# A hybrid attention and mixture-of-experts block on one core: twelve weight places, a loop over pairs of experts, and the second bias added in one piece

## The chip, the cores and the metric

The kernel runs on one core of one Trainium2 chip. The metric is the device time of one execution in microseconds (us); the median of the runs counts. A difference below 0.3%, some 3.3 us, can't be told from no change with runs of this kernel.

## The reference

The block has a front (two token mixers: causal pooling and sparse attention, gated and added to the input) and a mixture of experts over its result, followed by a last RMS norm with a gain. 256 tokens, width 1024, 32 experts, each token goes to 4 of them. The change lies in the experts:

```python
def moe(h, w_router, b_router, w1, b1, w2, b2):
    logits = hf @ w_router + b_router
    top_vals, top_idx = lax.top_k(logits, TOP_K_EXPERTS)
    gates = jax.nn.softmax(top_vals, axis=-1)
    combine = jnp.sum(jax.nn.one_hot(top_idx, N_EXPERTS) * gates[..., None], axis=1)
    out = jnp.zeros((b * s, d), jnp.float32)
    for e in range(N_EXPERTS):
        gu = hf @ w1[e] + b1[e]                      # w1[e]: 1024 x 2048, w2[e]: 1024 x 1024, float32
        g_ = jnp.minimum(gu[:, :D_FF], SWIGLU_LIMIT)
        u_ = jnp.clip(gu[:, D_FF:], -SWIGLU_LIMIT, SWIGLU_LIMIT)
        act = g_ * jax.nn.sigmoid(SWIGLU_ALPHA * g_) * (u_ + 1.0)
        out = out + combine[:, e:e + 1] * (act @ w2[e] + b2[e])
```

The weights of all experts are read whatever the router says: 32 times 12.58 MB, 402.7 MB of the 436 MB that the kernel reads.

## The kernel before, in words

**Experts as steps.** The tokens of an expert are gathered into 64 slots (one-hot columns from the router, times the tokens, on PE), so that an expert is 64 rows against its weights. Its weights come as 12 steps of 1 MB: 8 of the first matrix (`w1`, 8 MB, line 1517 on PE) and 4 of the second (`w2`, 4 MB, line 1566). Two steps are a chunk of 2 MB, and each chunk goes to a place in SBUF. PE counts `chunks_used` up by one when it is through a step.

**Between the two matrices** PE has small work while DVE and ACT make the activations of the expert (clamp, sigmoid, product): the transposes of the slot columns (1534), the gathering of half of the next pair's tokens (`gather`, 1404), the transposes of the activations (1547), the bias of the next first matrix (`bias1`, 1360). Behind the second matrix of every second expert, results go back from slots to tokens (`scatter`, lines 1149 to 1151): three products of f32r halves, high by high, low by high, high by low, for 4 blocks, 12 matmuls for a pair. The gate is in the slot columns `gpick` that the scatter uses. The second bias `b2` is added by one matmul of 32 rows (1526) in each of the first four experts, through `combT`, the transposed gates of the tokens, and `b2s`.

**Transfers.** All weights come through SP's queue, in the order of use. SP waits until PE has used the chunk that lies in a place, and then issues the next chunk for it, so each transfer is issued when its place comes free:

```python
sp.wait_ge(chunks_used, 2 * plan[c][2] + 2)
chunk(c // CHUNKS, c % CHUNKS, place[plan[c][0]], chunk_loaded[plan[c][0]])
```

There are 11 places of 2 MB. The first 12 experts (72 chunks) are written out, on every engine, in 2 MB chunks. Behind them SP loads `gfin`, the gain of the last norm, broadcast to all partitions (512 KB). Then a loop takes the 16 experts of groups 3 to 6, in transfers of 4 MB into 4 quads (16 MB), of which each is two places. The last group of 4 experts is written out again, in 2 MB chunks; the last expert's chunks are partly halved.

**The last expert** has an order of its own (`last_expert`): its first matrix at line 1460, its activations in two halves, its second matrix by columns at 1481, its scatter at 1488. Then come the sums of squares, the last norm and the output.

## Time and profile before

| | |
|---|---|
| runs, us | 1091.92, 1090.02, 1088.32; median 1090.02 |
| profiled execution, us | 1088.94 (1.08 below the median) |
| its span, us | 1087.2 (1.7 below its own time) |
| busy | PE 94%, DVE 30%, ACT 19%, POOL 1% |
| DMA over the span | 403 GB/s mean, 437.88 MB |

Times in rows and text are us from the start of the span. The front fills the first 175 us or so, the experts the rest, and the last 8.0 us, from the end of the last scatter, are the norm and the output.

### The profile page before, as it was taken

The numbers are of one execution on the slowest core, as the hardware profiler recorded it, in microseconds if no ns is written. First come the engines' busy times: TensorE is split into PE (matmuls) and PEld (weight loads), VectorE is DVE, ScalarE is ACT, GpSimd is POOL, SyncE is SP. The second block draws the span as 40 slices with busy tenths as digits, with TensorE's granted clock in tenths as the row PEclk, the third lists the DMA queues.
The fourth block names the chain that finished last, engine by engine and source line by source line (L and its number), as shares of the span: only waits on it lengthen the run. The fifth ranks groups of instructions, "written<-read, shape, count | busy, mean of one in ns | idle before, by whom it ended". The sixth has DMA issues, their size and how long they took to land.

```text
span 1087.2 us, 12200 instructions
## 1 busy us (share of the span) xinstructions
PE 1021.8 (94%) x4995; PEld 502.9 (46%) x4995; DVE 328.7 (30%) x724; ACT 201.2 (19%) x343; POOL 10.8 (1%) x14
## 2 busy tenths in 40 slices
PE   9999999999999999999989899898989898999896
PEld 7987785334343434343434343434343343434342
DVE  6966574222222222222122222121121221121223
ACT  6565642101110111011101110110010100110012
POOL 0000020000000000000000000000000000000000
PEclk9999999999999999999999999999999999999999
DMA  8786769999999999999999999999999999999994
GB/s 339 272 351 254 289 258 386 396 433 430 428 433 430 430 430 429 432 431 438 427 435 432 433 435 433 435 432 435 428 436 429 434 434 434 433 428 429 428 430 178
DMA packets 29719, 437.88 MB, mean 403 GB/s; under 512 B 4616, under 2 KB 5296, under 8 KB 7664
## 3 DMA queue, kind: packets, MB, share of 16 engines
q1 hardware_dynamic: 29392, 436.80, 94.9%
q8 instruction: 29, 0.48, 0.2%
q10 hardware_dynamic: 288, 0.52, 0.1%
q14 instruction: 10, 0.08, 0.0%
HBM read 436.26 MB, written 2.11 MB: 403 GB/s over the span
## 4 chain that ended last, share of the span: by engine, by line
PE 74%; DMA 21%; DVE 2%; issue 1%; ACT 1%; POOL 0%; SPq 0%; ACTq 0%; DVEq 0%; POOLq 0%
PE bank L1517 30%; DMA quad<-in_w 18%; PE bank L1566 15%; PE bank L1149 6%; PE bank L1150 5%; PE bank L1151 5%; PE bank L1404 3%; DMA place<-in_w 3%; PE bank L1360 1%; PE bank L1460 1%; PE bank L1547 1%; PE bank L1481 1%; PE bank L1306 0%; PE bank L1526 0%; PE bank L1488 0%
## 5 line engine op out<-in xcount | busy, mean ns | idle before, releaser
L1517 PE MATMUL bank<-quad,r 128*64 128x512 f32 x1024 | 236.9, 620 | 20.3 <-DMA quad<-in_w 20.2
L1517 PE MATMUL bank<-place,r 128*64 128x512 f32 x960 | 210.4, 594 | 5.2 <-DMA place<-in_w 5.2
L1517 PEld LDWEIGHTS bank<-quad,r 128*64 128x64 f32 x1024 | 79.8, 142 | 167.7 <-issue 163.1
L1026 DVE TENSOR_SCALAR r<-bank 128x512 f32<-128x512 f32 x32 | 22.1, 692 | 398.3 <-PE bank L1517 386.0
L1517 PEld LDWEIGHTS bank<-place,r 128*64 128x64 f32 x960 | 67.4, 137 | 137.9 <-issue 130.1
L1566 PE MATMUL bank<-quad,r 128*64 128x512 f32 x512 | 113.4, 595 | 8.6 <-issue 5.5
L1057 DVE TENSOR_TENSOR ysl<-bank,ysh 64x512 fp32r<-64x512 f32 x62 | 42.7, 689 | 254.9 <-ACT ysh L697 253.9
L1566 PE MATMUL bank<-place,r 128*64 128x512 f32 x480 | 106.3, 594 | 7.7 <-issue 7.0
L682 ACT ACTIVATE r<-r 128x512 f32<-128x512 f32 x31 | 19.6, 632 | 453.5 <-DVE r L1026 453.5
L697 ACT ACTIVATE ysh<-bank 64x512 fp32r<-64x512 f32 x62 | 36.6, 591 | 225.5 <-PE bank L1566 224.7
L749 DVE TENSOR_TENSOR wl<-ring,wh 128x1024 fp32r<-128x1024 f32 (+1 forms) x52 | 64.0, 1241 | 37.4 <-ACT wh L526 36.9
L1566 PEld LDWEIGHTS bank<-quad,r 128*64 128x64 f32 x512 | 40.8, 137 | 72.1 <-issue 72.1
L1566 PEld LDWEIGHTS bank<-place,r 128*64 128x64 f32 x480 | 39.6, 137 | 65.8 <-issue 65.1
L1404 PEld LDWEIGHTS bank<-rt,hs 128*128 128x128 f32 x528 | 61.5, 192 | 13.7 <-issue 12.9
L1404 PE MATMUL bank<-rt,hs 128*128 128x128 f32 x528 | 66.1, 278 | 0.0
L526 ACT ACTIVATE wh<-ring 128x1024 fp32r<-128x1024 f32 (+1 forms) x52 | 53.7, 1042 | 55.1 <-PE bank L1151 53.2
L1149 PE MATMUL bank<-wh,hTh 128*128 128x512 f32 x96 | 39.0, 406 | 0.0
L1150 PE MATMUL bank<-wl,hTh 128*128 128x512 f32 x96 | 37.6, 392 | 0.0
L1151 PE MATMUL bank<-wh,hTl 128*128 128x512 f32 x96 | 37.4, 390 | 0.0
L1547 PE MATMUL bank<-cst,r 128*128 128x128 f32 x124 | 19.4, 279 | 12.1 <-DVE r L1040 12.1
L691 ACT ACTIVATE r<-bank 128x512 f32<-128x512 f32 x31 | 18.5, 597 | 61.7 <-PE bank L1547 61.7
L1063 DVE TENSOR_TENSOR r<-bank,gcol 128x512 f32<-128x512 f32 x32 | 22.1, 691 | 23.2 <-PE bank L1404 22.6
(227 smaller groups left out, 851.2 us busy)
## 6 DMA issues: line engine op xcount, KB each, us to landing
quad<-in_w SPq DMA_DIRECT2D x48, 4096.0 KB, 29.4
place<-in_w SPq DMA_DIRECT2D x93, 2048.0 KB, 21.5
ring<-in_w_front SPq DMA_DIRECT2D x24, 1024.0 KB, 5.4
place<-in_w SPq DMA_DIRECT2D x2, 1024.0 KB, 33.7
place<-in_w_last SPq DMA_DIRECT2D x1, 2048.0 KB, 35.0
place<-in_w_last SPq DMA_DIRECT2D x2, 1024.0 KB, 33.7
ring<-in_w_idx SPq DMA_DIRECT2D x4, 384.0 KB, 5.5
xs<-in_x SPq DMA_DIRECT2D x2, 512.0 KB, 8.8
```

Source lines behind the costliest of these rows:

```text
L526: nc.scalar.activation(piece_cols(wh[n % LOOK], n), ring_piece(n), ACT.Copy).then_inc(high_ready, 1)
L697: nc.scalar.activation(ysh[own, c, :], YT[c * SLOTS:(c + 1) * SLOTS, :], ACT.Copy)\
L749: nc.vector.tensor_tensor(piece_cols(wl[n % LOOK], n), ring_piece(n), piece_cols(wh[n % LOOK], n).bitcast(f32), ALU.subtract)\
L1026: nc.vector.tensor_scalar(gclip, GA[:, :], LIMIT, None, ALU.min).then_inc(gclip_ready, 1)
L1057: nc.vector.tensor_tensor(ysl[c][own, :], YT[c * SLOTS:(c + 1) * SLOTS, :], ysh[own, c, :].bitcast(f32), ALU.subtract).then_inc(y_low, 1)
L1149: mm(o, ah, bh, start=start and first_in_bank, stop=False, skip_group_check=True)
L1150: mm(o, ah, bl, start=False, stop=False, skip_group_check=True)
L1151: return mm(o, al, bh, start=False, stop=stop, skip_group_check=True)
L1404: ins = mm(bk[:, k * P:(k + 1) * P], hs[:, b, d], pick[:, b, :], start=b == 0, stop=b == TB - 1)
L1517: ins = mm(bk[part, :], xgT[i // 2 % 2][:, k, own], w[:, c1:c1 + HALF], start=False, stop=k == KD - 1)
L1547: ins = nc.tensor.transpose(GA[:, c * P:(c + 1) * P], act[:, c * P:(c + 1) * P], ident)
L1566: ins = mm(YT[part, :], a_k, w[:, kk, c1:c1 + HALF], start=k == 0, stop=k == KD - 1)
```

## The change

- **Places and transfers.** Another layout of SBUF gives 12 places (24 MB), two to each of 6 quads. The first pair of experts comes in chunks of 2 MB, the pairs 1 to 14 in a loop with 4 MB transfers, on every engine; in the last pair, expert 30 has three transfers of 4 MB and expert 31 ten of 2, 1 and 0.5 MB (its first matrix by columns: `w1_last`). A transfer of 4 MB waits until its four steps are free (`place_free`).
- **Gain of the last norm.** The broadcast of 512 KB is gone from SP's queue. ACT's queue loads one row of 4.6 KB during the last pair, and two matmuls of one row (`final_factors`) spread it over the partitions.
- **Slots and gates.** The slot columns `pick` no longer hold the gate: PE makes the gate of each slot with eight matmuls of one column (`slot_gates`), and DVE multiplies it into the activations. The scatter then takes 4 matmuls an expert, with the high and low halves of the result stacked in 128 rows, between the matrices of the next expert.
- **Second bias.** All of it (8 matmuls of 32 rows by 256 columns, `second_bias`) stands in expert 0, between its matrices.
- **Order on PE.** `gather(0)` stands in the second expert of a pair ahead of the second matrix, `gather(1)` and the two first biases behind it. There is one buffer `xgT` in place of two. The transposed activations go to ACT in two halves.
- **Last expert.** Activations in two halves of columns, a scatter of 8 matmuls in f32r, first biases in float32 (`last_bias`).

```diff
-PLACES = 11
-GROUP = 4
-GROUPS = NE // GROUP
+PLACES = 12
 PAIRS = NE // 2
-QUADS = 4
-TURNS = GROUP * STEPS // 4 // QUADS
-FIRST = 3
...
+        first = [*o_early, o_hT, o_bias, o_gates, o_att, o_att + CHUNK, o_split, o_split + CHUNK, o_xs, o_late]
...
+        quad = [at(f"quad{q}", first[2 * q], 2 * CHUNK) for q in range(CHUNKS)]
+        place = [quad[c // 2][:, (c % 2) * CHUNK:(c % 2 + 1) * CHUNK] for c in range(PLACES)]
...
+            for c in range(5, PLACES):
+                for signal, n in former_use[c - 5]:
+                    sp.wait_ge(signal, n)
+                chunk(c // CHUNKS, c % CHUNKS, place[c], chunk_loaded[c])
+            def place_free(up, c):
+                sp.wait_ge(chunks_used, up * (2 * STEPS) + 2 * (c - PLACES + 1))
+            def load_pair(r, p):
+                for q in range(CHUNKS):
+                    place_free(r * PAIRS + p, 2 * q + 1)
+                    sp.dma_start(quad[q], w12[2 * p + q // 3, q % 3, :, :]).then_inc(quad_loaded[q], 16)
+            with sp.Fori(1, PAIRS - 1) as p:
+                load_pair(0, p)
+            for q in range(3):
+                place_free(PAIRS - 1, 2 * q + 1)
+                sp.dma_start(quad[q], w12[NE - 2, q, :, :]).then_inc(quad_loaded[q], 16)
+            for c in range(CHUNKS, PLACES):
+                i = c - CHUNKS
+                place_free(PAIRS - 1, c)
+                if i < 3:
+                    sp.dma_start(place[c], w1_last[i // 2, :, (i % 2) * CHUNK:(i % 2 + 1) * CHUNK]).then_inc(chunk_loaded[c], 16)
+                elif i < 5:
+                    src = w1_last[1, :, CHUNK:] if i == 3 else w12[NE - 1, 2, :, 0:CHUNK]
+                    sp.dma_start(place[c][:, 0:SLOT], src[:, 0:SLOT]).then_inc(chunk_loaded[c], 16)
+                    sp.dma_start(place[c][:, SLOT:CHUNK], src[:, SLOT:CHUNK]).then_inc(tail_loaded[i - 3], 16)
...
-            sp.wait_ge(chunks_used, gain_free)
-            sp.dma_start(gfin, final_norm.partition_broadcast(P)).then_inc(gfin_loaded, 16)
...
+                    nc.scalar.activation(GA[:, :], gclip, ACT.Sigmoid, scale=ALPHA).then_inc(sig_ready, 1)
+                    if i == 0:
+                        a.wait_ge(gT_done, up + 1)
+                        for half in (slice(0, SLOTS), slice(SLOTS, P)):
+                            nc.scalar.activation(gT[half, 0, :], YT[0:SLOTS, 0:SEQ], ACT.Copy).then_inc(gT_ready, 1)
+                    for h, bk in enumerate((GA, UA)):
+                        part = slice(h * SEQ, (h + 1) * SEQ)
+                        a.wait_ge(actT_done, 2 * u + h + 1)
+                        nc.scalar.activation(actT[:, part], bk[:, part], ACT.Copy).then_inc(actT_ready, 1)
...
+            with a.Fori(0, PAIRS - 1) as p:
+                expert_pair(0, p)
+            a.wait_ge(chunks_used, (PAIRS - 1) * (2 * STEPS) + 4)
+            nc.scalar.dma_start(gfin_row, final_row).then_inc(gfin_loaded, 16)
+            expert_pair(0, PAIRS - 1, final=True)
...
+                    if i == 0:
+                        v.wait_ge(gate_done, up + 1)
+                        nc.vector.tensor_copy(gate, GATHER[:, 0:2]).then_inc(slot_gate, 1)
+                        v.wait_ge(slot_gate, up + 1)
+                    v.wait_ge(sig_ready, u + 1)
+                    v.wait_ge(gu_ready, u + 1)
+                    nc.vector.scalar_tensor_tensor(out=act, in0=act, scalar=gate[:, i:i + 1], in1=GA[:, :],
+                                                   op0=ALU.mult, op1=ALU.mult).then_inc(act_ready, 1)
...
+            def scatter(u, i):
+                pe.wait_ge(y_low, 2 * u + 2)
                 for b in range(TB):
...
                     for c in range(2):
-                        three(YSUM[2 * b + c][:, :], gTh[:, t], gTl[:, t], ysh[:, c, :], ysl[c],
-                              False, True).then_inc(scattered, 1)
...
+            def slot_gates(up):
+                pe.wait_ge(pick_ready, up + 1)
+                for i in range(2):
+                    for b in range(TB):
+                        for part in (lo, hi):
+                            mm(GATHER[part, i:i + 1], own_pick(b, i), cpick[:, b, i:i + 1], start=b == 0, stop=b == TB - 1)
                 for b in range(TB):
...
+                    ins = nc.tensor.transpose(GATHER[lo, SEQ + b * P:SEQ + (b + 1) * P], own_pick(b, 1), ident)
+                ins.then_inc(gate_done, 1)
+            def slots_to_tokens():
+                for b in range(TB):
+                    ins = nc.tensor.transpose(YT[lo, b * P:(b + 1) * P], own_pick(b, 0), ident)
+                ins.then_inc(gT_done, 1)
+            def biases(n):
+                pe.wait_ge(sel_ready, n)
+                bias1(GA, bg)
+                bias1(UA, bu)
+            def second_bias():
+                pe.wait_ge(b2_loaded, 16)
+                pe.wait_ge(combT_ready, 4)
+                for n, q in enumerate((0, 2, 1, 3)):
+                    rows, c = slice(q * NE, (q + 1) * NE), (q % 2) * SEQ
+                    if n >= 2:
+                        pe.wait_ge(b2_added, 2 * n - 2)
+                    for b in range(TB):
+                        mm(YSUM[2 * b + q // 2][:, c:c + SEQ], combT[rows, b * P:(b + 1) * P], b2s[rows, :],
+                           start=False, stop=True, skip_group_check=True).then_inc(b2_added, 1)
+            def final_factors():
+                pe.wait_ge(gfin_loaded, 16)
+                for c, bk in enumerate((GATHER, UA)):
+                    mm(bk[:, :], gfin_row[:, D:D + P], gfin_row[:, c * HALF:(c + 1) * HALF],
+                       start=True, stop=True).then_inc(gfin_done, 1)
+            def last_bias(bk, rows):
+                for part, t in ((lo, bg), (hi, bu)):
+                    mm(bk[part, :], sel[rows, rows].bitcast(f32), t[rows, :].bitcast(f32), start=True, stop=False)
...
+                first_matrix(range(4))
+                pe.wait_ge(gfin_ready, 2)
+                last_bias(UA, hi)
+                scatter(u - 1, 0)
+                first_matrix(range(4, 6))
+                activations_turned(0)
...
+                if i == 0:
+                    slot_gates(r * PICKS + p)
+                if former:
+                    scatter(u - 1, 1 - i)
+                if i == 0:
+                    if opening:
+                        pe.wait_ge(combT_ready, 4)
+                    slots_to_tokens()
+                if opening:
+                    second_bias()
+                if i and not final:
+                    pe.wait_ge(gT_twice, 2 * up + 2)
+                    pe.wait_ge(pick_ready, r * PICKS + p + 2)
+                    gather(0)
+                pe.wait_ge(act_ready, u + 1)
+                for h, bk in enumerate((GA, UA)):
                     for c in (2 * h, 2 * h + 1):
                         ins = nc.tensor.transpose(bk[:, c * P:(c + 1) * P], act[:, c * P:(c + 1) * P], ident)
...
+                    ins.then_inc(actT_done, 1)
+                if i == 0:
+                    pe.wait_ge(gT_ready, 2 * up + 2)
                 for j in range(KD, STEPS):
...
+                    if j < KD + 2:
+                        pe.wait_ge(actT_ready, 2 * u + j - KD + 1)
+                    w = loaded_step(r, p, i, j).rearrange("p (k n) -> p k n", k=2)
                     for kk in range(2):
                         k = 2 * (j - KD) + kk
                         a_k = actT[:, (k % 4) * P + (k // 4) * SLOTS:(k % 4) * P + (k // 4 + 1) * SLOTS]
                         for part, c1 in ((lo, 0), (hi, HALF)):
                             ins = mm(YT[part, :], a_k, w[:, kk, c1:c1 + HALF], start=k == 0, stop=k == KD - 1)
                     ins.then_inc(chunks_used, 1)
...
+                if final:
+                    pe.wait_ge(gT_twice, 2 * up + 2)
+                    final_factors()
+                    pe.wait_ge(sel_ready, u + 2)
+                    last_bias(GA, lo)
+                    return
+                if i:
+                    pe.wait_ge(xgT_ready, r * HALVES + 2 * p + 3)
+                    gather(1)
+                biases(u + 2)
```

On **PE, in expert 0**, ahead of and between the two matrices. Before: the bias (1526), the slot transposes (1534), the gather (1404), the transposes of the activations (1547), the first bias (1360) and the second matrix (1566).

```order
L1517 MATMUL bank<-place_108,r_59 64x512 x7
L1526 MATMUL bank<-r_59 128x512 [waits b2_loaded,combT_ready]
L1534 MATMUL bank<-cst,rt 128x128 [waits gpick_ready]
L1534 MATMUL bank<-cst,rt 128x128
L1404 MATMUL bank<-rt,hs 128x128 [waits pick_ready]
L1404 MATMUL bank<-rt,hs 128x128 x7
L1547 MATMUL bank<-cst,r_59 128x128 [waits act_ready]
L1547 MATMUL bank<-cst,r_59 128x128 x3
L1360 MATMUL bank<-bu,sel 128x512 [waits sel_ready]
L1566 MATMUL bank<-place_109,r_59 64x512 [waits chunk_loaded4,actT_ready,gT_low]
L1566 MATMUL bank<-place_109,r_59 64x512 x7
```

After, with line numbers of the changed text: gate of the slots (1476, 1478), slot transposes (1484), second bias (1502), transposes of the activations (1629), the second matrix (1642).

```order
L1608 MATMUL bank<-quad_110,xgT 64x512 x7
L1476 MATMUL bank<-cpick,pick 64x1 [waits pick_ready]
L1476 MATMUL bank<-cpick,pick 64x1 x7
L1478 MATMUL bank<-cst,pick 64x128 x2
L1484 MATMUL bank<-cst,pick 64x128 [waits combT_ready]
L1484 MATMUL bank<-cst,pick 64x128
L1502 MATMUL bank<-b2s,combT 128x256 [waits combT_ready,b2_loaded]
L1502 MATMUL bank<-b2s,combT 128x256 x3
L1502 MATMUL bank<-b2s,combT 128x256 [waits b2_added]
L1502 MATMUL bank<-b2s,combT 128x256
L1502 MATMUL bank<-b2s,combT 128x256 [waits b2_added]
L1502 MATMUL bank<-b2s,combT 128x256
```

The gather and the first bias have left this place; the gates and seven more matmuls of second bias have come, of which two wait for others to be done.

On **SP's queue**, at the place where the first chunks are issued into places that PE has used. Before:

```order
L413 DMA r_59<-in_b 64x512
L350 DMA place_115<-in_w 128x4096 [waits x_ready]
L350 DMA place_105<-in_w 128x4096 [waits chunks_used]
L350 DMA place_106<-in_w 128x4096 [waits chunks_used]
L350 DMA place_107<-in_w 128x4096 [waits chunks_used]
L350 DMA place_108<-in_w 128x4096 [waits chunks_used]
L350 DMA place_109<-in_w 128x4096 [waits chunks_used]
```

After:

```order
L339 DMA quad_113<-in_w 128x4096 [waits piece_used] x2
L339 DMA quad_114<-in_w 128x4096 [waits x_ready]
L339 DMA quad_114<-in_w 128x4096 [waits piece_used]
L410 UNCONDITIONAL_BRANCH
L410 ISA
L408 ISA [waits chunks_used]
L408 DMA quad_109<-in_w 128x8192
L403 REGISTER_ALU
L408 ISA [waits chunks_used]
L408 DMA quad_110<-in_w 128x8192
L403 REGISTER_ALU
```

Each of the chunks waited for PE by itself; now two chunks are one transfer of 8192 columns with one wait, and a register operation of the loop stands between two of them.

On **PE, from the second matrix of expert 30** to the first matrix of expert 31. Before (`L1460` is the first matrix of expert 31):

```order
L1566 MATMUL bank<-place_105,r_59 64x512 [waits actT_ready,chunk_loaded0,gT2_ready,gT_low]
L1566 MATMUL bank<-place_105,r_59 64x512 x7
L1566 MATMUL bank<-place_106,r_59 64x512 [waits chunk_loaded1]
L1566 MATMUL bank<-place_106,r_59 64x512 x7
L1360 MATMUL bank<-bg,sel 128x512
L1460 MATMUL bank<-place_107,r_59 64x512 [waits chunk_loaded2]
L1460 MATMUL bank<-place_107,r_59 64x512 x7
```

After (`L1642` second matrix of expert 30, `L1509` the gain, `L1515` the float32 first bias, `L1532` the first matrix of expert 31, `L1467` the scatter of expert 30):

```order
L1642 MATMUL bank<-quad_111,gclip 64x512 x11
L1509 MATMUL bank<-gfin_row 128x512 [waits gfin_loaded,gT_twice]
L1509 MATMUL bank<-gfin_row 128x512
L1515 MATMUL bank<-bg,sel 64x512 [waits sel_ready]
L1515 MATMUL bank<-bu,sel 64x512
L1532 MATMUL bank<-quad_112,xgT 64x512 [waits chunk_loaded6]
L1532 MATMUL bank<-quad_112,xgT 64x512 x7
L1532 MATMUL bank<-quad_112,xgT 64x512 [waits chunk_loaded7]
L1532 MATMUL bank<-quad_112,xgT 64x512 x7
L1515 MATMUL bank<-bg,sel 64x512 [waits gfin_ready]
L1515 MATMUL bank<-bu,sel 64x512
L1467 MATMUL bank<-y,gT 128x512 [waits y_low]
```

The gain, four float32 bias matmuls and the scatter now stand ahead of or inside the first matrix of expert 31.

## Rows read from the trace of the kernel before

**Rows 1.** The page: the chain that ended last, by engine.

```profile
PE 74%; DMA 21%; DVE 2%; issue 1%; ACT 1%; POOL 0%; SPq 0%; ACTq 0%; DVEq 0%; POOLq 0%
```

**Rows 2.** Windows: us, busy (x) of PE, PEld, DVE, ACT, POOL, PEclk, DMA share, GB/s.

```profile
175.00:220.00 45.00, 44.31 (x219) 19.14 (x219) 11.81 (x41) 6.16 (x13) 0.00 (x0) 1.00 0.96 388
220.00:480.00 260.00, 252.19 (x1224) 108.13 (x1222) 61.83 (x135) 28.58 (x47) 0.00 (x0) 1.00 1.01 431
500.00:940.00 440.00, 405.08 (x1905) 173.58 (x1903) 95.26 (x209) 45.54 (x74) 0.00 (x0) 0.97 1.00 433
```

**Rows 3.** DMA issues at 205.5 and 212.9: line, size, us to landing.

```profile
place<-in_w SPq DMA_DIRECT2D x1, 2048.0 KB, 7.2
place<-in_w SPq DMA_DIRECT2D x1, 2048.0 KB, 9.5
```

**Rows 4.** DMA issues at 463.4, 463.9, 476.5 and 924.1.

```profile
place<-in_w SPq DMA_DIRECT2D x1, 2048.0 KB, 24.3
gfin<-in_final_norm SPq DMA_DIRECT2D x1, 512.0 KB, 25.0
quad<-in_w SPq DMA_DIRECT2D x1, 4096.0 KB, 22.2
quad<-in_w SPq DMA_DIRECT2D x1, 4096.0 KB, 29.6
```

**Rows 5.** DMA issues at 987.2 and 990.6, and the last, at 1037.06.

```profile
place<-in_w SPq DMA_DIRECT2D x1, 2048.0 KB, 29.9
place<-in_w SPq DMA_DIRECT2D x1, 2048.0 KB, 32.7
place<-in_w_last SPq DMA_DIRECT2D x1, 1024.0 KB, 34.8
```

**Rows 6.** The instruction-fetch queue in 220:490 and in 940:1072 (600:940 has none).

```profile
q8 instruction: 10, 0.16, 0.2%
q8 instruction: 4, 0.07, 0.2%
```

**Rows 7.** The chain at the opening: start us, us, what.

```profile
190.39 7.02 PE bank L1517 x32
197.40 1.05 PE bank L1526 x2
198.82 1.79 PE bank L1404 x16
201.78 7.09 PE bank L1566 x32
```

**Rows 8.** The chain of one pair in the steady part.

```profile
289.32 13.88 PE bank L1517 x64
303.64 0.23 PE bank L1150
330.83 0.69 DVE r L1026
342.60 2.72 PE bank L1517 x11
```

**Rows 9.** Waits of PE in 520:940: us in total, times, longest.

```profile
PE bank L1517 <- DMA quad<-in_w: 20.2, 12, 2.8
```

**Rows 10.** The chain of the tail.

```profile
998.06 34.88 DMA place<-in_w
1032.98 3.65 PE bank L1517 x16
1043.15 7.09 PE bank L1566 x32
1050.67 13.88 PE bank L1460 x64
1068.47 7.09 PE bank L1481 x32
1075.56 3.65 PE bank L1488 x8
```

More of the change, by code:

```diff
@@ L248, in hybrid_block @@
         chunk_loaded = [sem(f"chunk_loaded{i}") for i in range(PLACES)]
[L249 removed]
+        quad_loaded = [sem(f"quad_loaded{q}") for q in range(CHUNKS)]
         chunks_used = sem("chunks_used")
@@ L309, in hybrid_block @@
-        place = [at(f"place{i}", off, CHUNK) for i, off in enumerate(first)]
-        quad = [at(f"quad{i}", o_quads + 2 * i * CHUNK, 2 * CHUNK) for i in range(QUADS)]
-        order = [c % PLACES for c in range(END - 2 * QUADS)] + [0, 1, 2, 3, 6, 7, 8, 9]
-        plan = []
-        for c, i in enumerate(order):
-            uses = [n for n in range(c) if order[n] == i]
-            plan.append((i, len(uses) + 1, uses[-1] if uses else None))
-        halves = plan[END - 2 * QUADS:]
-        slots = [(first[halves[2 * n][0]] - o_quads) // (2 * CHUNK) for n in range(QUADS)]
@@ L320, in hybrid_block @@
-        assert sorted(slots) == list(range(QUADS))
-        for n, (i, _, _) in enumerate(halves):
-            assert first[i] == o_quads + (2 * slots[n // 2] + n % 2) * CHUNK
-        gain_free = 2 * (1 + max(c for c, i in enumerate(order) if first[i] == o_bias))
+        first = [*o_early, o_hT, o_bias, o_gates, o_att, o_att + CHUNK, o_split, o_split + CHUNK, o_xs, o_late]
+        assert len(first) == PLACES == 2 * CHUNKS and o_ring == o_att + SLOT and o_split == o_att + 2 * CHUNK
+        assert all(first[2 * q + 1] == first[2 * q] + CHUNK for q in range(CHUNKS))
@@ L325, in hybrid_block @@
+        lyl = [at(f"lyl{c}", first[4] + D + c * HALF, HALF, f32r) for c in range(2)]
+        junk = at("junk", first[5], TB * D).rearrange("p (b d) -> p b d", b=TB)
         block = ctx.enter_context(nc.Block())
@@ L403, in _ @@
                 ((x_ready, 4),),
+                ((piece_used, N_PIECES),),
             )
[L405 to L413 removed]
@@ L1433, in scatter, with loaded_step @@
-            def scatter(experts):
-                pe.wait_ge(y_low, 2 * experts)
+            def loaded_step(r, p, i, j):
+                n = i * CHUNKS + j // 2
+                if isinstance(p, int) and (p == 0 or i):
+                    if j % 2 == 0:
+                        pe.wait_ge(chunk_loaded[n], 32 if p else 16)
+                elif j % 4 == 0:
+                    short = 16 if i and not isinstance(r, int) else 0
+                    pe.wait_ge(quad_loaded[n // 2], (r * PAIRS + p) * 16 - short)
+                return place[n][:, (j % 2) * SLOT:(j % 2 + 1) * SLOT]
@@ new lines, in activations_turned, with second_matrix @@
+                def activations_turned(h):
+                    pe.wait_ge(last_act, h + 1)
+                    bk, part = (GATHER, UA)[h], (lo, hi)[h]
+                    for c in range(4):
+                        ins = nc.tensor.transpose(bk[:, c * SLOTS:(c + 1) * SLOTS], lact[part, c * P:(c + 1) * P],
+                                                  ident[part, part])
+                    ins.then_inc(lastT_done, 1)
+                def second_matrix(c, k, even, odd):
+                    for n, bk in enumerate((GATHER, GA) if c else (YT,)):
+                        cols = slice(n * SEQ, (n + 1) * SEQ) if c else slice(0, HALF)
+                        for part, kk, w in ((lo, k, even), (hi, k + 1, odd)):
+                            ins = mm(bk[part, 0:HALF // (1 + c)], actT[:, kk * SLOTS:(kk + 1) * SLOTS], w[:, cols],
+                                     start=k == 0, stop=k == KD - 2)
+                    return ins
@@ L1577, in _ @@
             gather_column(0, 3, YT).then_inc(gather_done, 1)
-            for e in range(FIRST * GROUP):
-                expert(0, e // GROUP, e % GROUP)
-            with pe.Fori(FIRST, GROUPS - 1) as g:
-                for i in range(GROUP):
-                    expert(0, g, i)
-            for i in range(GROUP - 1):
-                expert(0, GROUPS - 1, i)
+            expert(0, 0, 0, former=False, opening=True)
+            expert(0, 0, 1)
+            with pe.Fori(1, PAIRS - 1) as p:
+                for i in range(2):
+                    expert(0, p, i)
+            expert(0, PAIRS - 1, 0, final=True)
             last_expert()
```

649 lines of the change are left out of this document (294 added, 355 removed).

## The prediction

> **What bounds the kernel now.** The chain that ended last is three quarters PE and one fifth DMA [rows 1], which alone would make PE the bound. The windows say otherwise: from 220 on the 16 DMA engines are busy all the time at 431 to 433 GB/s, while PE has idle time, 405 us busy of 440 in the loop [rows 2]. One pair of experts takes PE 342.60 − 289.32 = 53.28 us [rows 8]. The DMA needs more for the same pair: the first 4 MB transfer of the loop lands at 476.45 + 22.2 = 498.65 and the last at 924.1 + 29.6 = 953.7, 47 transfers later [rows 4], so 9.68 us for each and 58.1 for the six of a pair. PE catches up and waits for quads 12 times, 20.2 us together [rows 9]. So between 220 and the last landing the time is bytes over bandwidth plus whatever makes the DMA pause; PE counts only at the opening (it frees the places) and in the tail, where the last transfer lands at 1037.06 + 34.8 = 1071.86 [rows 5] and PE ends its last scatter at 1079.21, with hardly a pause since 1032.98 [rows 10].
>
> The transfers are not equally fast. Before the loop, chunk 17 lands at 212.9 + 9.5 = 222.4 [rows 3] and chunk 71 at 463.4 + 24.3 = 487.7 [rows 4]: 265.3 us for 54 chunks, 4.91 us each, where half of 9.68 is 4.84. After the loop, from 953.7 to 1071.86, 24 chunks take 118.2 us, 4.92 each. Two neighbours show where it goes: 1017.1 and 1023.3 [rows 5], 6.2 us apart, 1.4 too many. In both stretches instructions are fetched, 10 and 4 blocks, and in the loop none [rows 6]. Whether 2 MB transfers or the fetches are at fault, I can't tell from this; the change removes both from most of the span.
>
> **The opening, +0.9 us.** A 4 MB transfer needs four free steps. The third of them (chunks 16 and 17) waits for all 12 steps of expert 0, so for the end of its second matrix. Before, PE ends steps 4 to 7 at 197.41 and begins the second matrix at 201.78 [rows 7], and chunk 17 is issued only after that matrix and two steps of expert 1. In the changed order what stands in the gap is: gates and slot transposes (no matmul of one column is in the trace: at least nothing, at most the 1.79 / 8 = 0.22 us of a gather matmul for each of the eight [rows 7], plus 0.4 for transposes; I take 2.0 together, near the top, because eight separate small instructions are nearer to eight small matmuls than to none), the second bias, and the turn through the activations' transposes, ACT's copy and the start of the matrix, 1.3 us (201.78 less the gather's end, 200.61, is 1.17, and the copy is now split). The second bias: one matmul of 512 columns took 1.05 [rows 7], so eight of 256 take 4.2 at most; at the pace of the f32r products (0.23 for 512 columns [rows 8]) 0.9 at least; the weights' matmuls, 32 of 512 columns that run in pairs on the two halves of PE, so 16 slots in 13.88 us [rows 8], give 0.87 for 512 columns and 3.4 for the eight, which I take: they are float32 too, and the row of 1.05 comes behind matmuls of another shape. The second matrix then ends at 197.4 + 2.0 + 3.4 + 1.3 + 7.09 = 211.2. A 2 MB transfer issued at 205.5 needed 7.2 us [rows 3], a 4 MB one 4.84 more: chunk 17 lands at 223.3 in place of 222.4. The bounds: −1.4, if the gap is as long as DVE's four operations of 0.69 [rows 8] and the turn, and +3, if the bias takes 4.2 and PE waits a microsecond for the gates. PE waits for no data in this stretch, so an earlier landing of chunks 12 to 15 gains nothing.
>
> **The steady part, −5.7 us.** From chunk 17 on before needs 1071.86 − 222.4 = 849.4 us. After it are 84 transfers of 4 MB (81 of the loop, 3 of expert 30) at 9.68, 813.3 us, and six chunks' worth for expert 31 at 4.92, 29.5: 842.8. The written-out last pair may still have a pause of 1.4 or none; with 0.9 for it, 843.7. Of the difference of 5.7, 1.2 are the gain: its broadcast landed at 463.9 + 25.0 = 488.9, 1.2 behind chunk 71 [rows 4], and now it's a row of a few KB on another queue. If the pauses all stay, 1.2 is what is left; if all go, −6.6. [...]
>
> That PE keeps up is a condition of this. Its pair becomes 2 × (13.88 + 7.09) = 41.9 for the matrices, some 5.2 between those of the even expert (2.0, four scatter matmuls of 0.23, DVE's chain, the turn) and 4.4 in the odd one, 1.8 for the gather behind the second matrix and 1.7 for two times two biases: 55, against 58.1. The scatter saves four f32r matmuls a pair, 0.9, but the gates and the gather's new place take more. It is hidden by 3 us a pair.
>
> **The tail, +3.1 us.** I count from the landing of the last part of expert 30's first matrix, 998.06 + 34.88 = 1032.94 [rows 10]; behind it the same bytes follow, so this landing is tied to the last one. Before: 3.65 for the last two steps, 6.52 to the second matrix (1036.63 to 1043.15), 7.09, 0.43 for the bias, 13.88, 3.92 to the second matrix of expert 31 (1064.55 to 1068.47), 7.09, 3.65 for the last scatter: 46.2 [rows 10]. After: the half matrix lands as one 4 MB transfer, and PE has four steps to do, 6.94 (+3.3). Between the matrices 5.2 (−1.3). Gain and float32 first biases in front of expert 31: two matmuls of 512 columns 1.7, two on half the columns of PE 0.9 to 1.7, taken as 1.3, less the 0.43 of before (+2.6). The first matrix has a bias of 0.9 and a scatter of 1.1 inside, and 0.6 of transposes in front of the second, in place of 3.92 (−1.3). The last scatter is eight f32r matmuls, with DVE's last halves in front of it 3.5 (−0.15). Sum 49.3. The bounds are +1 (the float32 biases at 0.43, the gap at 4.5, the scatter at 2.2) and +5 (each wait for DVE and ACT halves a microsecond longer). The norm and the output stay at 8.0.
>
> **Sum.** 0.9 − 5.7 + 3.1 = −1.7. Against the profiled execution of 1088.94 that is 1087.2; this one lay 1.08 below the median, so 1088.3 for the median. The bounds of the three terms give its own range, 1085.5 to 1091.5.
>
> **The rivals.** *More is given back than lost* (0.37): no pause is left (−6.6), the gap of the opening is as long as the DVE chain (−1.4) and the tail adds its lower bound or a bit more (+2.5): −5.5, 1084.5. For it speaks that no row of the loop shows a pause; against it that the tail's 4 MB transfer is certain to make 3.3 us of PE work later.
> *PE becomes the bound* (0.06): slower. In the middle of the pair each small matmul, transpose and copy waits for another engine: gates, DVE's copy of the gate, its product, the copy on ACT in two halves, and the single buffer for gathered tokens, which must be read before it is written. From 3 us more than my 55 a pair the DMA waits for PE, and every microsecond beyond costs 15. At 60 us a pair: 15 × 1.9 = 28, 1117. Against it: these chains add up to 5.2 from rows of 0.69 and 0.23, and before PE never fell back in the loop.
> *The tail takes over 6 us more* (0.05): last-expert work waits for DVE in order, h by h, and the DVE's pieces are on half the partitions with the duration of the whole: 1088.3 + 4 to 6, so 1092 to 1095.
> [...]
> *The change does nothing where the time is* (within my own forecast): with pauses left as they were, −1.2 + 0.9 + 3.1 = +2.8, 1092.8.
>
> **How the numbers follow.** My forecast with its range has 0.51. The prediction is 1088.3. Faster by over 0.3% is below 1086.7: the first rival and a little of the forecast's lower end, 0.38. Slower is above 1093.3: the PE and tail rivals and a rest of the pauses' case, 0.12. The rest, 0.50, is the same. For 8 in 10 the range must hold the first rival with 2 us below it, and the case of unchanged pauses: 1082.5 to 1093.0.
>
> **What will show it.** Chunk 17's landing (as the third 4 MB transfer) near 223 and its issue near 211; 9.68 between 4 MB transfers from there to expert 31, without the 1.4 us steps; no 512 KB transfer; PE's pair at 55 and waits for quads, each pair, of some 3 us; the last landing near 1067; and 49 us from the last landing of expert 30's first matrix to the end of the last scatter. It is wrong if quads land further apart than 9.7 (then PE or the pauses), if PE never waits for a quad in the loop, or if the tail comes out at 46 or 52.

## The result, and the profile after

The changed kernel takes 1090.72 us in the median (13 runs, 1088.24 to 1092.28), the kernel before 1088.87 beside it (13 runs): ratio 1.0017, 95% interval 1.0009 to 1.0024. So it is slower by 1.85 us, and the interval lies above 1; the forecast had 1.7 us less. This is under the 0.3% that was said at the start to be lost in noise: with 5 to 27 runs of a kernel the intervals are some 0.1% to either side, and differences are read by them here. The profiled execution took 1090.24, its span is 1088.4, against 1087.2 before.

The chain that ended last, on the page of the changed kernel, by engine, beside [rows 1]:

```profile
PE 77%; DMA 9%; DVE 6%; another core or an unknown queue 3%; issue 2%; ACT 2%; DVEq 0%; ACTq 0%; SPq 0%
```

The windows beside [rows 2] (us, busy (x) of PE, PEld, DVE, ACT, POOL, PEclk, DMA share, GB/s):

```profile
175.00:220.00 45.00, 44.49 (x236) 19.54 (x237) 13.27 (x48) 8.09 (x17) 0.00 (x0) 1.00 0.97 393
220.00:480.00 260.00, 251.53 (x1304) 103.23 (x1302) 59.45 (x130) 34.62 (x65) 0.00 (x0) 1.00 1.00 432
500.00:940.00 440.00, 394.28 (x2020) 161.46 (x2018) 91.38 (x201) 53.49 (x100) 0.00 (x0) 1.00 1.00 432
```

The DMA is still busy all the time, but in the loop it moves 432 GB/s where it moved 433, and that with PE idle for longer. The 4 MB transfers in the middle of the loop show it: issued at 297.50 and at 963.12, the second 71 transfers behind the first (line, size, us to landing):

```profile
quad<-in_w SPq DMA_DIRECT2D x1, 4096.0 KB, 24.0
quad<-in_w SPq DMA_DIRECT2D x1, 4096.0 KB, 48.0
```

They land at 321.5 and 1011.1: (1011.1 − 321.5) / 71 = 9.71 us each, where the loop before had 9.68 [rows 4]. At the opening, the issues at 188.27, 198.34 and 209.61, of chunks 12 to 17, two at a time:

```profile
quad<-in_w SPq DMA_DIRECT2D x1, 4096.0 KB, 14.6
quad<-in_w SPq DMA_DIRECT2D x1, 4096.0 KB, 14.7
quad<-in_w SPq DMA_DIRECT2D x1, 4096.0 KB, 14.8
```

Chunk 17 comes at 209.61 + 14.8 = 224.4, 2.0 us later than before [rows 3], though its transfer was issued 3.3 us earlier. The chain there, beside [rows 7]:

```profile
191.14 7.01 PE bank L1608 x32
198.15 0.41 PE bank L1476 x15
198.56 0.34 PE bank L1478 x2
...
199.12 1.11 PE bank L1502 x8
...
200.24 1.21 PE bank L1502 x8
...
202.34 7.09 PE bank L1642 x32
```

The gates (1476, 1478), the slot transposes and the second bias (1502) take 3.3 us (198.15 to 201.45) and the second matrix begins at 202.34, only 0.56 later than before. PE's waits in 500:940 (us, times, longest), beside [rows 9], whose stretch is 520:940 (over 500:940 the row of before is the same):

```profile
PE bank L1608 <- DMA quad<-in_w: 32.7, 21, 2.6
```

PE waits longer and more often than before, so it isn't behind. Blocks of instructions fetched in 220:490 and in 940:1072 are 3 and 2, for 10 and 4 in [rows 6]; in 600:940 there are none:

```profile
q8 instruction: 3, 0.05, 0.1%
q8 instruction: 2, 0.03, 0.1%
```

And the end, beside [rows 10]:

```profile
1001.47 8.81 PE bank L1608 x32
...
1023.68 7.02 PE bank L1608 x32
...
1030.70 7.10 PE bank L1608 x32
...
1041.74 7.09 PE bank L1642 x32
1048.83 1.91 PE bank L1509 x4
1050.74 1.01 PE bank L1515 x4
1051.75 7.02 PE bank L1532 x32
...
1072.85 3.68 PE bank L1549 x24
...
1076.56 0.39 ACT lyh L701
...
1078.84 1.29 DVE hs L1142 x2
```

The last 4 MB of expert 30's first matrix were issued at 979.54 and land 51.0 us later, at 1030.57; PE is through the four steps ahead of it at 1030.70. The last weights that PE waits for are those that land at 1001.42, in expert 29; from there to the end of the matrices it waits only for DVE and ACT. The last row shown is the first product of the last norm; the span ends at 1088.4.

**Where the 1.2 us of the span went**, from these rows: to chunk 17, 224.41 for 222.44, +2.0; from there to the landing of expert 30's first matrix, 1030.57 − 224.41 = 806.2 for 1032.94 − 222.44 = 810.5, −4.3; from there to the end, 1088.4 − 1030.57 = 57.8 for 1087.2 − 1032.94 = 54.3, +3.5.

### The profile page after: what moved, and what is told of

Its sections match the earlier page's. It is cut to its first block, busy times and chain, and to the rows that moved or that the text cites. A ratio compares the mean times of both kernels' runs of the same rounds, so it can differ in the third digit from the quotient of the medians.

```text
span 1088.4 us, 12952 instructions
## 1 busy us (share of the span) xinstructions
PE 1010.6 (93%) x5235; PEld 485.4 (45%) x5235; DVE 324.3 (30%) x712; ACT 221.3 (20%) x402; POOL 10.8 (1%) x14
## 4 chain that ended last, share of the span: by engine, by line
PE 77%; DMA 9%; DVE 6%; another core or an unknown queue 3%; issue 2%; ACT 2%; DVEq 0%; ACTq 0%; SPq 0%
PE bank L1608 36%; PE bank L1642 18%; DMA quad<-in_w 9%; PE bank L1180 4%; PE bank L1182 4%; PE bank L1181 4%; PE bank L1437 3%; DVE act L1049 2%; DVE act L1039 2%; PE bank L1391 1%; PE bank L1532 1%; PE bank L1629 1%; DVE act L1041 1%; DVE gclip L1038 1%
## 5 line engine op out<-in xcount | busy, mean ns | idle before, releaser
L1608 PE MATMUL bank<-quad,xgT 128*64 128x512 f32 x1984 | 440.1, 598 | 38.5 <-DMA quad<-in_w 38.5
L1608 PEld LDWEIGHTS bank<-quad,xgT 128*64 128x64 f32 x1984 | 142.8, 137 | 319.5 <-issue 281.2
L1642 PE MATMUL bank<-quad,gclip 128*64 128x512 f32 x992 | 219.7, 595 | 8.0 <-ACT gclip L680 7.4
L1642 PEld LDWEIGHTS bank<-quad,gclip 128*64 128x64 f32 x992 | 69.4, 137 | 138.4 <-issue 124.1
L1062 DVE TENSOR_TENSOR y<-bank,y 64x512 fp32r<-64x512 f32 x62 | 42.7, 689 | 224.5 <-ACT y L683 223.6
L683 ACT ACTIVATE y<-bank 64x512 fp32r<-64x512 f32 x62 | 36.7, 592 | 215.1 <-PE bank L1642 214.4
L1437 PEld LDWEIGHTS bank<-pick,hs 128*128 128x128 f32 x512 | 60.7, 191 | 15.1 <-issue 13.0
L1437 PE MATMUL bank<-pick,hs 128*128 128x128 f32 x512 | 64.1, 278 | 0.0
L1467 PE MATMUL bank<-y,gT 128*128 128x512 f32 x124 | 36.8, 418 | 0.0
L1467 PEld LDWEIGHTS bank<-y,gT 128*128 128x128 f32 x124 | 20.9, 188 | 15.8 <-issue 13.0
L1049 DVE SCALAR_TENSOR_TENSOR act<-act,gate,bank 128x512 f32<-128x512 f32 x31 | 23.2, 748 | 2.9
```

The source lines that it names most:

```text
L1049: nc.vector.scalar_tensor_tensor(out=act, in0=act, scalar=gate[:, i:i + 1], in1=GA[:, :], op0=ALU.mult, op1=ALU.mult).then_inc(act_ready, 1)
L1062: nc.vector.tensor_tensor(y[SLOTS:P, c, :], YT[c * SLOTS:(c + 1) * SLOTS, :], y[0:SLOTS, c, :].bitcast(f32), ALU.subtract).then_inc(y_low, 1)
L1437: ins = mm(bk[:, k * P:(k + 1) * P], hs[:, b, d], pick[:, b, :], start=b == 0, stop=b == TB - 1)
L1467: mm(YSUM[2 * b + c][:, :], gT[:, i, b * P:(b + 1) * P], y[:, c, :], start=False, stop=True, skip_group_check=True).then_inc(scattered, 1)
L1608: ins = mm(bk[part, :], xgT[:, k, own], w[:, c1:c1 + HALF], start=False, stop=k == KD - 1)
L1642: ins = mm(YT[part, :], a_k, w[:, kk, c1:c1 + HALF], start=k == 0, stop=k == KD - 1)
```

## The experiments

Ratios are against the kernel before, in runs on the same chip, with 95% intervals; the changed kernel's is 1.0017. Theory: the transfers are slower for two reasons that the prediction didn't have, their address and the four free steps with long delivery at the opening. Rivals: PE's longer work between the matrices, PE as the bound, more transfers in flight.

**The address of the places.** The change also moved the places. Before, they begin at byte 48640 of a partition, a multiple of 512; afterwards the layout rounds to 128 bytes, and they begin at 32640, 384 bytes behind one. The first run moves them to a multiple of 512 (small tensors moved to make room):

```diff
-        o_quads = -(-top[0] // 32) * 32
+        o_quads = top[0] + -(base // 4 + top[0]) % 128
-        eexp = new("eexp", TB * NE).rearrange("p (b e) -> p b e", b=2)
+        eexp = at("eexp", o_s + 2848, TB * NE).rearrange("p (b e) -> p b e", b=2)
...
+        gate = at("gate", o_s + 3584, 2)
```

> The changed kernel with its places moved 384 bytes down, so that all begin at a multiple of 512 bytes, as those of the kernel before do (the changed kernel's lie 384 bytes behind one). Theory, the pace depends on the address: 4 MB transfers of the loop land 9.68 us apart in place of 9.71, 84 of them save 2.6 us, about 1088.1 us. Rival, the pace comes from something else in the change (more transfers waiting, the order of sources): 9.71 stays and so does the time, 1090.7.

Measured: 1088.33 us, ratio 0.9999 (0.9990 to 1.0008), 2 us below the changed kernel. The issues at 298.01 and 961.48, again 71 transfers apart:

```profile
quad<-in_w SPq DMA_DIRECT2D x1, 4096.0 KB, 23.9
quad<-in_w SPq DMA_DIRECT2D x1, 4096.0 KB, 47.8
```

(961.48 + 47.8 − 298.01 − 23.9) / 71 = 9.68. Then the other way round, the kernel before with its places 384 bytes up:

```diff
+        top[0] += 96
         o_quads = top[0]
```

> The kernel before with its places moved 384 bytes up, nothing else. Theory, the address: transfers of its loop land 9.71 us apart in place of 9.68, the rest slower by the same share, so some 2.5 us more, 1091.4. Rival: 9.68 and 1088.9 as before.

Measured: 1093.25 us, ratio 1.0046 (1.0032 to 1.0060), 4.6 us more, about twice what was expected. Its issues at 477.40 and 926.95, 47 transfers apart, give 9.72:

```profile
quad<-in_w SPq DMA_DIRECT2D x1, 4096.0 KB, 24.1
quad<-in_w SPq DMA_DIRECT2D x1, 4096.0 KB, 31.5
```

Its 2 MB transfers lost more: by the landings in the trace 4.89 us apart, for 4.85 before (73 and 72 undisturbed spacings), so 0.8% where the 4 MB ones lose 0.3%; the expectation had used the same share for both. Two theories of the pace fall with these two runs: neither the number of transfers in flight nor the order of sources was touched. Which multiple counts, from three more places of the same kernel, 256, 128 and 64 bytes behind a multiple of 512 (the number at the end of the line that sets `o_quads` is 64, 32 or 16 floats):

```diff
-        o_quads = top[0] + -(base // 4 + top[0]) % 128
+        o_quads = top[0] + -(base // 4 + top[0]) % 128 + 64
```

> The changed kernel with its places 256 bytes behind a multiple of 512. By the theory of the address, if it is the multiple of 512 that counts, 4 MB transfers land 9.71 us apart as with 384 bytes; if a multiple of 256 is enough, 9.68. Profile only.

> The changed kernel with its places 128 bytes behind a multiple of 512. Since 0 and 256 bytes gave 9.68 between 4 MB transfers and 384 gave 9.71: 9.71 if a multiple of 256 counts, 9.68 if 384 alone is slow. Profile only.

> The changed kernel with its places 64 bytes behind a multiple of 512: 9.71 by the rule of 256 bytes, or slower still if each halving of the multiple costs. Profile only.

Issues at 297.94 and 961.03 with 256 bytes:

```profile
quad<-in_w SPq DMA_DIRECT2D x1, 4096.0 KB, 23.5
quad<-in_w SPq DMA_DIRECT2D x1, 4096.0 KB, 47.8
```

and at 297.46 and 964.95 with 128 bytes:

```profile
quad<-in_w SPq DMA_DIRECT2D x1, 4096.0 KB, 25.9
quad<-in_w SPq DMA_DIRECT2D x1, 4096.0 KB, 48.0
```

That is 9.68 and 9.71, and with 64 bytes 9.71 too, from 298.19 + 23.0 to 962.84 + 48.0. So of the five places the two at a multiple of 256 bytes have 9.68 and the three off it 9.71, and how far it is missed makes no difference. The times (1087.32, 1092.38 and 1089.63 us) are of one execution each and decide nothing; the spacings do. That is 0.3% more at 64, 128 and 384 bytes off alike; why, no run shows.

**The opening.** The second pair in 2 MB transfers, each issued when its own two steps are free:

```diff
+            for c in range(PLACES):
+                place_free(1, c)
+                chunk(2 + c // CHUNKS, c % CHUNKS, place[c], chunk_loaded[c])
-            with sp.Fori(1, PAIRS - 1) as p:
+            with sp.Fori(2, PAIRS - 1) as p:
```

> The changed kernel with the weights of its second pair in 2 MB transfers, each issued when its own two steps are free; the loop begins with the third pair. Theory, the opening is lost because a 4 MB transfer waits for four steps and then needs 14.7 us with little queued ahead of it: chunk 17 lands near 222.4 in place of 224.4, 2 us less, 1088.7. Rival, the longer work between the matrices of expert 0 (gates, second bias) holds the places: chunk 17 lands near 224 still and the time stays at 1090.7.

Measured: 1088.62 us, ratio 0.9994 (0.9985 to 1.0003), 2.1 us below the changed kernel by the medians and 2.5 by the ratios, for the 2 expected. Chunk 17, issued at 209.63 as it was in the changed kernel, lands at 221.0, not 224.4:

```profile
quad<-in_w SPq DMA_DIRECT2D x1, 2048.0 KB, 11.4
```

Its place was free no earlier, so it isn't the work between the matrices; the transfers ahead of it had come in time. The rival by itself, with the second bias behind the second matrix of expert 0 (ACT waits for it before it overwrites `combT`):

```diff
                 if opening:
                     second_bias()
-                if i and not final:
...
+                if opening:
+                    second_bias()
                 if final:
```

> The changed kernel with the eight second-bias matmuls behind the second matrix of expert 0, where they hold back no transfer of its first 12 steps. By the first theory of the opening (4 MB transfers that come late) the third 4 MB transfer is issued 2.3 us earlier, near 207.3, but waits for the one ahead that lands at 213.0: it lands near 222.7, 1.7 us less, about 1089.0. By the rival (the work between the matrices alone) it is 2.3 us less. If the opening is hidden somewhere, no change from 1090.7.

Measured: 1091.04 us, ratio 1.0021 (1.0012 to 1.0030). No gain: the third case of the expectation came, and both theories fail in one point. The third transfer was not issued 2.3 us earlier but at 209.49, and lands 14.8 later:

```profile
quad<-in_w SPq DMA_DIRECT2D x1, 4096.0 KB, 14.8
```

In the chain of this run the second matrix begins at 202.21, for 202.34 with the bias ahead of it, and waits for DVE's last product; the bias then stands by itself on PE's path:

```profile
200.45 0.76 DVE act L1050
...
202.21 7.09 PE bank L1641 x32
209.30 1.11 PE bank L1503 x8
```

So the second bias was hidden all the time, under the activations that DVE and ACT make meanwhile.

**PE's room.** One gather more for each pair in the loop, which writes the same values again:

```diff
+                    if not isinstance(p, int):
+                        for k in range(4):
+                            gather_column(1, k)
                     gather(1)
```

> The changed kernel with one gather more on PE behind the second matrix of each odd expert in the loop; it writes the same values once more, 1.8 to 2.0 us a pair. Theory, the loop is bound by the transfers, and PE has 5 us a pair to spare (52.9 of 58.3): waits for quads become shorter and the time stays at 1090.7. Rival, PE or the time at which it frees places sets the pace: 14 pairs by 1.9, 27 us more.

Measured: 1091.74 us, ratio 1.0020 (1.0011 to 1.0030), the changed kernel's to within its interval, with more work on PE. Its waits for quads in 500:940 fell from the 32.7 us shown above:

```profile
PE bank L1608 <- DMA quad<-in_w: 11.0, 7, 2.6
```

PE as the bound, the rival that was to cost 28 us, is out: a pair takes PE 474.43 − 421.56 = 52.9 us in the changed kernel (two starts of an odd expert's first matrix), against 58.3 of transfers.

**The end.** First the second 4 MB of expert 30's first matrix in two:

```diff
             for q in range(3):
+                if q == 1:
+                    for c in (2, 3):
+                        place_free(PAIRS - 1, c)
+                        chunk(NE - 2, c, place[c], chunk_loaded[c])
+                    continue
```

> The changed kernel with the second 4 MB of expert 30's first matrix in two 2 MB transfers. Theory, PE sets the end from the landing of these 4 MB on, and their size adds the 3.3 us of PE work that come after it: the first 2 MB are worked on while the second land, 3.3 us less, about 1087.4. Rival, the last landing or a wait further back sets the end and the 4 MB are hidden: 1090.7.

Measured: 1089.52 us, ratio 1.0004 (0.9995 to 1.0013): some 1.4 us, not 3.3, and the interval overlaps the changed kernel's. PE comes to expert 30 straight from a late 4 MB transfer of expert 29, which lands at 1001.42 in the changed kernel and is followed by 8.81 us for its four steps, so the first half of the pair of transfers lies there unused. By the trace even the 1.4 isn't there: from that landing to the end of the span it is 1090.3 − 1003.58 = 86.7 us in this run and 1088.4 − 1001.42 = 87.0 in the changed kernel. Then the pair before in 2 MB as well (the loop is one turn shorter, on PE as on SP):

```diff
-            with sp.Fori(1, PAIRS - 1) as p:
+            with sp.Fori(1, PAIRS - 2) as p:
                 load_pair(0, p)
+            for c in range(PLACES):
+                place_free(PAIRS - 2, c)
+                chunk(NE - 4 + c // CHUNKS, c % CHUNKS, place[c], chunk_loaded[c])
```

> The changed kernel with all weights of the pair before the last, and the second 4 MB of expert 30's first matrix, in 2 MB transfers. Theory, after the run that halved expert 30's transfer alone: PE comes to it without a pause from the last 4 MB transfer that it waited for, in expert 29, so both must be halved. Then PE is at expert 30 early, waits for its last 2 MB and has 3.3 us less to do behind it: about 1087.4. Rival, PE's order of work in the last pairs sets the end whatever the transfers: 1089.5, as with expert 30 alone.

Measured: 1090.18 us, ratio 1.0011 (1.0002 to 1.0020). No better: PE now waits for expert 30's first 4 MB, which land at 1021.49. It then takes 15.48 us for the matrix and 8.71 for the first half of expert 31's, for 14.1 and 7.02 in the changed kernel, at a mean granted clock of 0.90 and 0.80 (1.00 over the same work there):

```profile
1021.62 15.48 PE bank L1618 x64
...
1051.20 8.71 PE bank L1542 x32
```

Expert 30's first 4 MB in two as well:

```diff
-                if q == 1:
-                    for c in (2, 3):
+                if q < 2:
+                    for c in (2 * q, 2 * q + 1):
```

> As the run with the last pairs in 2 MB, with the first 4 MB of expert 30 in two transfers too. Theory: PE could not be early at expert 30's second 4 MB because its first 4 MB came as one, at 1021.5, and 13.9 us of work follow. Now the last 2 MB of the matrix (1031.3) has 3.65 us behind it, PE ends the matrix near 1035 in place of 1037.8: 2.9 us less than the changed kernel, 1087.8. Rival: each wait of PE is followed by matmuls at the lower granted clock (8.8 us for 7.0), and the shorter waits give back what the smaller transfers gain: 1089.5 to 1090.5.

Measured: 1091.89 us, ratio 1.0029 (1.0017 to 1.0041), no faster than the changed kernel. The first matrix ends at 1034.18 as expected, and then PE waits 2.35 us for the 4 MB of the second matrix, which lands at 1040.17, and takes 8.56 us for it, at a granted clock of 0.82 on the mean:

```profile
1030.50 3.68 PE bank L1618 x16
...
1037.82 2.35 another core or an unknown queue
...
1040.31 8.56 PE bank L1652 x32
```

It ends at 1048.87, and in the changed kernel, which began later, at 1048.83. Last, the second matrix in two:

```diff
-                if q < 2:
+                if q < 3:
```

> As the last run of this kind, with expert 30's second matrix in two transfers as well. Theory, after the trace of that run: what was gained at the first matrix was lost at the second, whose 4 MB land as one at 1040.3, and PE then works on them for 8.6 us at the lower clock. In two transfers the first half is there at 1035.4, the matrix begins near 1037.9 and ends near 1045 in place of 1048.8: 3.9 us less than the changed kernel, 1086.8. Rival: waits and clock take the gain again, 1090 to 1092.

Measured: 1088.31 us, ratio 0.9992 (0.9983 to 1.0001), 2.7 us below the changed kernel by the ratios (0.25%); 3.9 were expected. After the same 3.68 us the second matrix now begins without a wait for its weights and runs at a granted clock of 1.00:

```profile
1032.26 3.68 PE bank L1618 x16
...
1039.88 7.09 PE bank L1652 x32
```

The 4.0 us between this run and the last (by the ratios) are near the 2.35 of the wait and the 1.5 of the slow matrix. So expert 30's three 4 MB transfers and the pair before formed a row of waits of nearly the same end, and taking one away showed the next.

**Together**, with the edits shown above: aligned places, the second pair in 2 MB, and as much of the end in 2 MB as in the run named: with the second transfer of expert 30 alone, with the pair before, with the whole first matrix, and with all of expert 30.

> The changed kernel with three things together: places at multiples of 512 bytes, the second pair in 2 MB transfers, the second 4 MB of expert 30's first matrix in two transfers. If the three causes are separate, their gains add up: 2.4 and 2.1 as measured and 3.3 as expected, 7.8 us less than 1090.7, about 1082.9, below both kernels. If two of them are the same microseconds, 1085 or more.

> Places at multiples of 512 bytes, and 2 MB transfers for the second pair, the pair before the last and the second 4 MB of expert 30's first matrix. If the gain at the end adds to the other two: 2 us less than the 1085.4 with expert 30's alone, 1083.4. If the faster transfers have already moved the end onto PE: 1085.4.

> Places at multiples of 512 bytes, 2 MB transfers for the second pair, the pair before the last and all of expert 30's first matrix. By the theory of the end 2.9 us less than the same kernel without the last two (1085.4), 1082.5; by the rival 1085.5.

> Places at multiples of 512 bytes, 2 MB transfers for the second pair, the pair before the last and all of expert 30. If the three causes are now each removed: 2.4 + 2.1 + 3.9 less than 1090.7, 1082.3. By the rival, as the run without the halved second matrix, 1086.9 to 1085.4.

Measured, in this order: 1085.40 us, ratio 0.9966 (0.9954 to 0.9978); 1085.65, 0.9962 (0.9949 to 0.9975); 1086.89, 0.9980 (0.9971 to 0.9989); 1083.01, 0.9941 (0.9928 to 0.9955). One of the six executions of the second took 2089.17 us, for a reason that isn't on record; the ratio is without it, and the other five have a median of 1085.15. The steps at the end repeat what they did alone, the third giving back and the fourth gaining most. The last is the fastest of all, 6.4 us below the kernel before and 8.3 below the changed one (1.0017 − 0.9941 = 0.76%); the three parts measured alone, 2.0, 2.5 and 2.7 by their ratios, add up to 7.2.

## Why the prediction was wrong

Three of its readings held: the transfers bound the kernel from the opening to the pair before the last, PE has room in the loop, and the time is the sum of an opening, a steady part and a tail. Two sizes in that sum were off, both in the transfers and both in the same direction; a third, the norm and the output, was taken as unchanged and wasn't.

**The opening, +0.9: the step that failed is "a 2 MB transfer issued at 205.5 needed 7.2 us [rows 3], a 4 MB one 4.84 more".** The 4 MB ones needed 14.6 to 14.8 us with at most one other ahead of them, twice 7.2, not 7.2 + 4.84 = 12.0. By luck part of these 2.8 us was hidden: the second matrix ended and the transfer was issued 1.6 us earlier than the forecast of 211.2, as the gates and the bias cost nothing beyond DVE's chain, so +2.0 came out for +0.9. With the cause removed (2 MB in the second pair) the run gained 2.5 us. The small work of expert 0, on which half of that paragraph was spent, decided nothing: the row to read was DVE's chain of 0.7 us each [rows 8], which was there as the lower bound.

**The steady part, −5.7: the step that failed is "84 transfers of 4 MB at 9.68".** They took 9.71, because their places begin at another address. Up to expert 30's first matrix there are 83 of them, by the forecast 803.4 us and measured 806.2; the difference is 83 × 0.033 = 2.7 us, more than the whole miss at the opening, and the aligned run gave 2.0 us back. A pace read from a trace belongs to the addresses it was measured with, and the prediction took it as a property of the chip; the layout was in the change (`o_quads`) and was not read. Spacings above 9.7 were named as a sign of being wrong, but put down to PE or the pauses, and it was neither. The paragraph also measured this term to the last landing, and the tail from an earlier one. To the same landing the forecast is −7.1, and −4.3 came: 2.8 too little, of which this slip happened to hide 1.4.

**The pauses** came out as forecast in this trace, in part by luck. From 224 to 1040 no spacing of the changed kernel's 4 MB transfers is above 9.72 us, so the steps of 1.4 are gone, with the one allowed for the last pair (0.9). But by the landings in the traces of its 15 variants, nine have one step of 1.1 to 1.8 us (11.25 us at 284.5 with the places 128 bytes off, for instance); the kernel before and its shifted one have three each, of 1.4 to 1.6. The size of the transfers isn't their cause: steps come with 4 MB as with 2 MB, and the run with the last pairs in 2 MB has 17 spacings of 2 MB, none late. Each of these steps has the fetch of a block of instructions within its spacing, but most fetches make no step: the changed kernel's trace has four between 224 and 1046, and none. And that in the loop before none are fetched, as the prediction has it, holds for 600:940 alone; in 490:600 there are four, and no spacing above 9.89:

```profile
q8 instruction: 4, 0.07, 0.2%
```

That the fetches make the steps is argued from this; no run removed them alone.

**The tail, +3.1, measured +3.5,** is near in sum by luck. Its start is not a landing that PE waits for: PE runs on from 1001.42. To the end of the last scatter matmul, 1078.59 + 0.39 = 1078.98, it is 48.4 for 46.2, so +2.2. The other 1.4 are the step "the norm and the output stay at 8.0": they take 1088.4 − 1078.98 = 9.4. The last of the sums of squares on ACT begins 0.6 us behind that matmul, where before it began at its end (1079.22 for 1079.21); what the rest is stays open.

```profile
1078.59 0.39 PE L1584 MATMUL bank<-lyl,gT 128*128 128x512 f32 x1
1079.57 0.60 ACT L499 ACTIVATE junk<-bank 128x512 f32<-128x512 f32 x1
```

The gap between the matrices is 3.9 us (1037.80 to 1041.74) for the 5.2 taken; the gain and the float32 biases 1.91 + 1.01 for 1.7 + 1.3; from the end of the last product of expert 31's second matrix to the end of the span it is 1088.4 − 1076.53 = 11.9, and 3.5 + 8.0 were taken. That the last 4 MB cost 3.3 us is not borne out: halving them alone was worth 1.4 at most, and the whole of the 4 MB transfers at the end 2.7.

**The rivals.** PE as the bound is excluded by its waits and by the run with more work on PE. Nor does the number of transfers count: they land 9.68 us apart with 4 MB and 4.85 with 2 MB in the kernel before, so a fixed cost that adds to the spacing is some 0.02 us at most (2 × 4.85 − 9.68). The faster case lacked the address as all others did: with the address, the opening and the end put right, the same change gives 1083.0, near the 1084.5 of that case.

In numbers: −1.7 was forecast for the span and +1.2 came; +1.1 of the difference is the opening, +1.4 the steady part as it was counted, −0.9 the tail up to the last scatter and +1.4 the norm and the output. The bounds of the three terms add up to −7.0 and +6.8, 1083.0 to 1096.8; the range that the prediction gives from them, 1085.5 to 1091.5, is narrower and not worked out.

## What to carry to other kernels

Where transfers bound a kernel, a new layout is part of the change: look at where each destination begins, and count a pace read from a trace only for the alignment that it was measured with (here 9.71 us for 9.68, 2.0 us of the time). The large transfers of this case cost nothing in the steady part (9.68 us for 4 MB, 4.85 for 2 MB), but 2.5 us at the opening and 2.7 at the end: at the opening they waited for all of their place and then took 14.6 to 14.8 us to come, and at the end all the work on them, 7.0 to 8.8 us, was left when they landed. Halving one of several late transfers showed only the next (1.4 us at most for one, 2.7 for all of them), so look at the row of them before judging the first.

## What the runs showed of the hardware

- Transfers of 4 MB into rows of 32 KB were 0.3% slower when the rows began off a multiple of 256 bytes in SBUF (9.71 us apart at 64, 128 and 384 bytes behind a multiple of 512, 9.68 at 0 and 256), those of 2 MB, with rows of 16 KB, 0.8% (4.89 for 4.85; 384 bytes off).
- With at most one other queued ahead, the 4 MB transfers issued from 188.27 to 209.61 in the changed kernel took 14.6 to 14.8 us to land, the 2 MB ones issued from 187.37 to 212.92 in the kernel before 7.2 to 10.4; behind the opening they land 9.7 and 4.85 to 4.9 us apart. So the 432 GB/s of the loop were reached with transfers that overlap, and not at the opening (393 GB/s in 175:220).
- Some waits of PE of 2.4 to 2.6 us were followed by matmuls that took 8.6 to 8.8 us where others took 7.0 to 7.1. Two places in the chain of the changed kernel show it: behind the same wait the four steps take 7.11 us at a granted clock of 1.00 in the first (593.5:600.6), and 8.81 at 0.81 on the mean in the second (943.2:952.0). The 8.71 us of expert 31 shown above, at 0.80, have no such wait just ahead, but the gain's matmuls and the float32 biases; behind the same matmuls the changed kernel takes 7.02. What tells the cases apart stays open.

```profile
590.90 2.58 another core or an unknown queue
...
593.52 7.11 PE bank L1608 x32
...
940.56 2.58 another core or an unknown queue
...
943.19 8.81 PE bank L1608 x32
```
